# Raw inputs for more chunks ahead of three kinds of norm in a five-layer fp32 transformer kernel

## What is computed

```python
for layer in range(4):
    h = rmsnorm(x, attn_norm[layer])
    m = attention(h, ...)            # diff, stick-breaking, sliding window, diff
    x = x + m @ w_o[layer]
    h = rmsnorm(x, ffn_norm[layer])
    x = x + conv_gated_ffn(h, w_up, conv_w, conv_b, w_down)
x = rmsnorm(x, final_norm)
# the fifth layer
h = rms_norm(x, g_mix_pre); ...
y = concatenate([y_pool, y_attn]) @ w_out
x = x + rms_norm(y, g_mix_post)
h = rms_norm(x, g_ffn_pre)
x = x + rms_norm(conv_ffn(h, ...), g_ffn_post)
x = x + (p @ w_ple) * sigmoid(x @ w_ple_gate)
```

## Time and profile before

| | |
|---|---|
| median of 3 runs | 1525.98 us (1525.39 to 1526.9) |
| the profiled execution's own time | 1525.59 us |
| its span, first to last instruction | 1524.0 us |
| PE busy | 1497.7 us, 98% of the span |
| DVE busy | 1048.0 us, 69% |
| ACT busy | 870.3 us, 57% |
| POOL busy | 328.9 us, 22% |

### The profile page before, as it was taken

One profiled execution on the slowest core, in us unless ns is written; L12 is line 12 of the kernel. 1 busy time (PEld: TensorE's weight loads), 2 busy tenths in 40 slices (PEclk: granted clock), 3 DMA queues, 4 the chain that ended last, 5 costly groups with the idle time before them and its releaser, 6 DMA issues.

```text
span 1524.0 us, 28435 instructions
## 1 busy us (share of the span) xinstructions
PE 1497.7 (98%) x11572; PEld 1428.5 (94%) x11572; DVE 1048.0 (69%) x1690; ACT 870.3 (57%) x1380; POOL 328.9 (22%) x482
## 2 busy tenths in 40 slices
PE   8999999999999999999999999999999998999998
PEld 7999999899999998989999899999998897999998
DVE  6668877564368775686877566678775767665545
ACT  5776655456547554584755446767564566554443
POOL 2102212213232222212121221022222361222100
PEclk9999999999999999999999999999999999999999
DMA  6643655444326555561655545436555555265450
GB/s 252 209 153 128 236 191 199 175 160 157 111 88 231 208 171 194 177 210 53 221 197 191 193 155 191 152 130 230 194 185 179 180 177 194 84 221 172 171 217 29
DMA packets 39598, 265.42 MB, mean 174 GB/s; under 512 B 5215, under 2 KB 5530, under 8 KB 8752
## 3 DMA queue, kind: packets, MB, share of 16 engines
...
## 4 chain that ended last, share of the span: by engine, by line
PE 83%; DVE 9%; ACT 5%; issue 2%; DMA 0%; POOL 0%; ACTq 0%; DVEq 0%; POOLq 0%
PE bank L1547 21%; PE bank L1548 20%; PE bank L1549 20%; PE bank L1558 8%; PE bank L1557 4%; DVE w_lo L863 4%; PE bank L1596 3%; ACT w_hi L367 2%; DVE tmp L909 2%; PE bank L1605 1%; PE bank L1741 1%; DVE acc L897 1%; PE bank L1730 1%; ACT sq L388 1%; PE bank L1722 1%
## 5 line engine op out<-in xcount | busy, mean ns | idle before, releaser
L863 DVE TENSOR_TENSOR w_lo<-w_raw,w_hi 128x2048 fp32r<-128x2048 f32 x240 | 554.0, 2314 | 93.0 <-ACT w_hi L367 90.9
L1547 PE MATMUL bank<-h_hi,w_hi 128*128 128x256 f32 x2032 | 579.5, 285 | 1.7 <-DVE w_lo L863 1.7
L1548 PE MATMUL bank<-h_lo,w_hi 128*128 128x256 f32 x2032 | 574.9, 283 | 0.0
L1549 PE MATMUL bank<-h_hi,w_lo 128*128 128x256 f32 x2032 | 574.9, 283 | 0.0
L367 ACT CAST w_hi<-w_raw 128x2048 fp32r<-128x2048 f32 x240 | 454.8, 1904 | 68.3 <-DMA w_raw<-w_std 47.6
L1547 PEld LDWEIGHTS bank<-h_hi,w_hi 128*128 128x128 f32 x2032 | 389.6, 192 | 7.3 <-issue 4.2
L1548 PEld LDWEIGHTS bank<-h_lo,w_hi 128*128 128x128 f32 x2032 | 389.7, 192 | 0.1
L1549 PEld LDWEIGHTS bank<-h_hi,w_lo 128*128 128x128 f32 x2032 | 389.6, 192 | 0.0
L1558 PE MATMUL bank<-act_both,w_hi 128*128 128x512 f32 x672 | 239.0, 399 | 0.0
L1318 DVE SCALAR_TENSOR_TENSOR tmp<-bank,par,tmp 128x255 f32<-128x255 f32 (+1 forms) x362 | 156.4, 478 | 108.2 <-ACT tmp L798 107.1
L798 ACT ACTIVATE tmp<-bank,par 128x256 f32<-128x256 f32 x181 | 93.2, 560 | 179.3 <-PE bank L1549 179.3
...
## 6 DMA issues: line engine op xcount, KB each, us to landing
w_raw<-w_std SPq DMA_DIRECT2D x240, 1024.0 KB, 4.8
...
```

Source lines behind the costliest of these rows:

```text
L863: dve.tensor_tensor(w_lo[:, n % SLOTS, :], w_raw[:, n % RAW, :], w_hi[:, n % SLOTS, :].bitcast(F32), ALU.subtract).then_inc(lo_ready, 1)
L1547: pe.matmul(dst, wh, xh, start=first, stop=False, skip_group_check=shared)
L1548: pe.matmul(dst, wh, xl, start=False, stop=False, skip_group_check=shared)
L1549: done = pe.matmul(dst, wl, xh, start=False, stop=last, skip_group_check=shared)
```

## The change

It does three things, and moves what depends on them.

- **The start.** Chunks 0, 1 and 2 are all raw. Chunk 1 arrives and is split in two halves (`second_split`), the statistic moves from chunk 0 into chunk 1, behind its first tile, and chunk 2, whose rows are positions, gets its factor as a number per partition (`row_rstd`, `evac_rows`). The bias vectors stand behind the fourth tile of chunk 0. The small numbers of the first layer (`lam`) are summed by one tiny matmul. `first_layer` orders DVE's work by hand: the first scores are taken before chunk 1's outputs are scaled, and the first division stands ahead of the split of chunk 4. The normalised tiles are due at chunk 3. `project_half` waits for each of them there.
- **Layers 0 to 3.** Up chunks 0 and 1 are raw, with the statistic behind the fifth tile of up chunk 0; the norm's parts are due at up chunk 2. DVE writes all eight `hf` tiles, then splits up chunk 2, and only then writes the four even `h_lo`. The outputs of up chunk 1 are scaled like those of up chunk 0.
- **Layer 4.** Up chunk 0 is run in two parts (`two_parts`): old `x` times gain, and `y` times both gains (`mixed_hi`, `mixed_lo`), each 48 matmuls, into the two halves of the banks. DVE puts `mix_rstd` on the second, adds, and puts `rstd` on the sum. The square sums go through DVE's `acc`, and PE sums them behind the fifth tile of the second part.

The core of the diff:

```diff
 def split_h(app):
-    act.wait_ge(used, first_chunk[app] + 1)
+    act.wait_ge(used, first_chunk[app] + raw_chunks(app))   # 3, 2 (layers 0-3), 1
@@ ACT, layer 4, for each tile of wo4
+    act.mul(mixed_hi[:, t, :], source[:, (t - a) * S:(t - a + 1) * S],
+            mixed_gains[:, t:t + 1]).then_inc(mixed_high, 1)
@@ ACT, wo: raw_high(app, k) now in layer 4 too, ahead of squared(3)
-    if layer < 4:
-        for k in tiles:
-            raw_high(app, k)
+    for k in tiles:
+        raw_high(app, k)
@@ DVE normalise
-                    if k % 2 and k > 1:
+                    if k % 2 and k > 1 and behind is None:
                         low(k - 3)
+                if behind is not None:
+                    behind()
+                    for k in (0, 2, 4):
+                        low(k)
                 low(DT - 2)
@@ DVE, wo of layers 0 to 3
-                        normalise(app, SUMS[name][2])
-                        ahead(c0 + 1, AHEAD)
+                        normalise(app, SUMS[name][2], lambda: ahead(c0 + 1, AHEAD))
@@ DVE, up: which chunks get rstd on their outputs
-                        first = isinstance(j, int) and j == 0
+                        first = j < (2 if ffn < 4 else 1)
@@ PE, up
-                    for k in range(2):
+                    if layer == 4:
+                        two_parts(c0, app)
+                    kinds = ((prev, False), ("raw", True), (None, True)) if layer < 4 else (None, (None, True))
@@ PE, where the statistic stands
-                    elif raw is not None and k == {"d": 1, "w": 2}.get(raw[0], 5):
+                    elif raw not in (None, "x", "raw") and k == {"d": 1, "w": 4}.get(raw[0], 5):
                         statistic(raw)
```

More of the change, by code:

```diff
@@ L358, in _ @@
         def _(act):
[L359 removed]
+            split = [2]
             def split_to(c):
@@ L1650, in project_half @@
                     chunk_ready(c)
-                done = outputs(weight_slot(layer, c), tile, pj[slot][:, tile * S:tile * S + S])
+                for k in range(DT):
+                    if c == RING and tile == 0:
+                        pe.wait_ge(h_hi_done, k + 1)
+                        pe.wait_ge(h_lo_odd if k % 2 else h_lo_even, k // 2 + 1)
+                    done = product(pj[slot][:, tile * S:tile * S + S],
+                                   [w_tile(weight_slot(layer, c), k, 2 * P, tile * P)], [h_tile(k)],
+                                   k == 0, k == DT - 1)
                 if tile:
```

357 lines of the change are left out of this document (236 added, 121 removed).

## The result

| | before | after |
|---|---|---|
| median, lowest to highest | 1526.28 us (1525.39 to 1526.9, 4 runs) | 1513.28 us (1512.18 to 1513.59, 4 runs) |
| the profiled execution | 1525.59 us, span 1524.0 | 1513.59 us, span 1512.0 |

The ratio is 0.9915, with a 95% interval of 0.9904 to 0.9927: 13.0 us faster. The forecast was 6.05 us faster (1519.5 us); the time measured lies within the range given, and next to the time of rival 1 (1512.5 us).

A forecast was written before the change was run, and what follows sets the result against it. PE, busy 98% of the span, was taken as the bound, with losses at three places. Gains of 4.4 and 3.85 less 2.2 us made 6.05 us, from 1525.59 to 1519.5 us; range 1512 to 1523.5 us.

The forecast's parts named there:

- rival 1: Layers 0 to 3: POOL costs DVE nothing in the new order, 1.2 us won per layer, 1512.5 us; 16%.
- Part A: The start: PE begins chunk 4's products at 38.8 instead of 42.9 us; 4.4 us won, including less DMA.
- The 0.3 us for fewer bytes ahead of the weights: The start: 0.7 MB less of DMA ahead of the weights wins 0.3 us.
- Part B: Layers 0 to 3, up chunks: 0.55 us lost per layer, 2.2 us in four.
- I take the same 0.5 us for each: Layers 0 to 3: each of POOL's four `h_lo` costs DVE 0.5 us in the changed order as well.
- the joined wait ahead of up chunk 3: Layers 0 to 3: PE's three small waits become one of 1.4 to 2 us before up chunk 3.
- The second term: Layers 0 to 3: ACT's cast, then DVE's split, of up chunk 4 come later; 0.55 us lost per layer.
- The sign for it: Layers 0 to 3: forecast wrong if DVE's split of up chunk 2 takes 2.3 us and PE does not wait.
- Part C: Layer 4: up chunk 2 starts at 1307.5 us; 3.85 us won after paying 5.76 us for 48 added matmuls.
- if ACT holds the statistic of `wo4` by over 1 us: Layer 4: forecast wrong if ACT delays the statistic of `wo4` by over 1 us.
- Rivals 2: The start's gain is given back by the end of layer 0's attention, 1523.9 us; 10%.
- 3: Layers 0 to 3: each joined wait drops the clock, costing 3 us four times, 1531.5 us; 4%.

The follow-up runs named there:

- after_again: The changed kernel unedited, measured once more among the experiments: 1514.47 us, ratio 0.9929 to the kernel before.
- inter: The changed kernel with DVE's old order in layers 0 to 3 (`h_lo` between the `hf`, split of up chunk 2 last): 1525.45 us, ratio 1.0002.

## Why the prediction was right or wrong

1. **What bounds the kernel**: right. All that was won is PE's idle or slow time at the three places.
2. **Part A, 4.4 us**: right. 4.6 and, in after_again, 42.89 - 38.08 = 4.8 us. Chunk 4 starts at 38.34, forecast 38.8, behind a wait for `w_lo` as foretold. That DVE's split of chunk 4 comes last was the right step, and its chain holds row by row: the first `hf` at 19.32 (forecast 19.65), that split from 36.01 (36.4). The 0.3 us for fewer bytes ahead of the weights are shown by no run on their own. What it left out is the transfer of the bias rows, due 7.5 us earlier than before (DVE at 29.9 in place of 37.4), which takes up to 2.2 us in some executions.
3. **Part B, -2.2 us**: wrong in sign, +5.2 measured. The failed step is "I take the same 0.5 us for each". The runs showed 0.5 us in the old order (2.03 for four) and 0.14 in the new (0.56 for four). This alone moves the joined wait ahead of up chunk 3 by 1.5 us per layer: forecast 1.4 to 2 us, measured 0.42. The second term, up chunk 4 late by 0.55 us, was too large as well: PE starts it at 149.30, 5.99 us after up chunk 3, so 0.23 us are lost. The two together are 1.8 us per layer, and -0.55 + 1.8 = 1.25 against 1.3 measured. That the three waits join into one ahead of up chunk 3, and that the split there is late next, was right.
4. **Rival 1** (POOL costs DVE nothing, 1512.5 us) gave the time, and its mechanism is what the trace shows: the long split holds and POOL stands. The sign for it was to be that DVE's split of up chunk 2 takes 2.3 us and PE does not wait: it took 2.28, and PE waits 0.42. That the time comes so near is in part luck, since part C fell 1.5 us short in this profile. It got 16%, because the forecast took its price from the earlier trace rows, which are rows of the old order, in which DVE works without a gap until the taps.
5. **Part C, 3.85 us**: right in size where the weights land as before (3.8 us in after_again). In the profile of the result it was 2.3. The forecast put the statistic of `wo4` 0.35 us late. Counted from the row of L1871, ACT takes it 1.65 us late in the first profile, through a chunk that landed 2.4 us late ahead of ACT's queue, and 0.1 us late in after_again. So the sign "if ACT holds the statistic of `wo4` by over 1 us" did come, and the lower bound of 2 us allowed for it. From ACT's last square (1277.20) to up chunk 2 (1299.21) it takes 22.0 us, as forecast.
6. **Rivals 2 and 3**: the start's lead was not given back. A joined wait that drops the clock did not occur in the changed kernel, where the wait was 0.42 us. In inter, with 2.50 us per layer, the clock fell behind it in two of four layers, for 1.7 us each, where the rival had 3 us in every one.
7. The sum of A, B and C in the first profile is 4.6 + 5.2 + 2.3 = 12.1 us, against 12.0 by the spans.

On the Trainium skill's rule for the shared port (SBUF — State Buffer, Who interferes with whom), which the prediction weighed: POOL's `h_lo` of 3.9 us beside DVE's split agrees with DVE holding it. That each instruction holds for its own length and no longer does not fit by itself, since DVE ran the split and three `h_lo` while POOL's one stood. No run here shows what decides who goes next.
